# Expert gates placed among the late blocks of the first table, and three regroupings in a second block

## The chip, the cores and the metric

One core of a Trainium2 chip. The metric is device time in microseconds (us) for one execution, the median of three. TensorE is PE in the profile (PEld its weight loads), VectorE is DVE, ScalarE is ACT, GpSimd is POOL, SyncE is SP.

## What is computed

Two transformer-like blocks over 256 tokens of width 1024, all in float32. The first ends in a feed-forward part with 16,384 experts: each token takes 8 x 16 of them, and an expert is a pair of keys (i1, i2), each of 0 to 127.

```python
expert = i1 * N_KEYS + i2
gate = jax.nn.softmax(best_s, axis=-1)
act = jax.nn.gelu(jnp.einsum('nd,ned->ne', hx, u[expert]))
return jnp.einsum('ne,ned->nd', gate * act, v[expert])
```

The second begins with one projection `h @ w_in` that is cut into a recurrent branch (`rx`, `rgate`, 2 x 1344 columns), sparse attention's q, k and v, its 48 gate columns `nsa_g` (3 for each of 16 heads, through a sigmoid), and two mixing gates. Sparse attention also compresses windows of 32 positions: `gelu((windows + pe) @ w1) @ w2`, for k and for v.

## The kernel before, in words

**Weights** come as one stream of 512 KB quarters through a ring of four (`ring`). SP loads a quarter when its slot is free. For most of them ACT rounds it to float32r (`round_quarter`, L824, its instruction L829), POOL takes the rest (`lower_quarter`, L1687), and PE multiplies three products: high by high, high by low, low by high (`product`, L318, instructions L323 to L325). SPLIT names the quarters treated so; others are multiplied as float32 (L321).

**The expert part** computes all experts for all tokens. The first table (u) is 128 quarters, called blocks: block m holds the experts with i2 = m, i1 on partitions, and `peer_u` (L613) multiplies it with all 256 tokens, 24 matmuls of 256 columns. Two blocks fill one PSUM bank, four banks (0 to 3) go round, and ACT's `gelu_u` (L962, L968) takes a bank to `region`, which holds activations [i1, block, token]. Beside the first U_EARLY = 80 blocks DVE finds each token's 128 slots (top keys, top pairs; L1390 to L1427); ACT's exponential for the softmax (L980) stands behind those 80 blocks on ACT's queue. Then PE turns the slots (L632), so that i1, i2 and the gate lie [slot, token] in banks 6 and 7, DVE copies them to `slotT` (L1432), and the other 48 blocks follow.

Only then come the **gates**, in 64 groups of 4 tokens. For a token a 128 x 128 matrix of gates is a matmul (float32, L646) of a one-hot matrix of i1 (ACT: four squares L991 and a relu L995) with one of i2 times the gate (DVE, L1444). DVE multiplies the result into `region` (`weigh`, L1453). X serves as buffer for the one-hot matrices; it is written out to HBM before and read back after.

Then the second table (v), 128 blocks: ACT rounds the activations (L1010), DVE takes the rest (L1476), PE multiplies (`peer_v`, L656).

**The second block.** 32 recurrent blocks of 84 columns (`feature_major`, L462, 24 matmuls of 256 columns each); the last two carry 24 gate columns each, which PE multiplies token-major (L323 to L325 with 24 columns) into bank 7. Then nine blocks z0 to z8 of 512 columns (`z2`, L722; `token_major`, L443, 48 matmuls each), which ACT keeps (L1082). After z5, ACT takes the sigmoid of the gates (L1092) and squares q and k (L1096 to L1098), DVE sums them (L1535), ACT takes the root (L1100), DVE scales q into N2 (L1544), and PE turns it (`transposes`, L420, instruction L425). The same buffer is filled and turned for k during z6 (L1554) and for the compressed k and v during z7 (L1562). After z8 PE multiplies the compression weights with the windows (L747, 60 columns: 4 groups of 15 windows) and separately with the position vector (L751, 1 column).

Every engine works through its own queue in the order written; waits are on semaphores.

## Time and profile before

| | |
|---|---|
| median of three runs | 1992.43 us (1988.84 to 1996.98) |
| the profiled execution | 1988.24 us, span 1986.5 us |
| PE busy | 1684.7 us, 85% of the span |
| DVE busy | 1091.3 us, 55% |
| ACT busy | 889.9 us, 45% |
| POOL busy | 1143.9 us, 58% |
| weights streamed | 536 quarters of 512 KB |

The span is the time from the first to the last instruction; the execution's own time has 1.7 us more around it. Matmuls overlap, so PE's busy time tells when it has work, and the pace is read from counts over a stretch. The granted clock of TensorE is a share of 2.4 GHz: 1.00 or 0.50 at any moment, a mean over a stretch. A releaser (`<-`) is what ended the idle time in front of an instruction.

### The profile page before, as it was taken

The page shows a single profiled execution, that of the slowest core. Times are in us where ns is not written, and L with a number is a line of the kernel's source. Part 1 is how long each engine was busy: PE and PEld are TensorE (multiplying, and loading weights), DVE is VectorE, ACT ScalarE, POOL GpSimd, SP SyncE. Part 2 cuts the span into 40 slices and gives each one's busy share as a digit, 9 for nine tenths or more (in the row PEclk, how much of TensorE's full clock was granted, in tenths as well). Part 3 has the DMA queues.
Part 4 walks back from the last instruction along what each step waited for, and adds up shares of the span by engine and source line. Part 5 has one row for each costly group of instructions (what it writes and reads, how often), then busy time and mean ns, then how long its engine had stood idle before and what let it go on. Part 6 is the DMA issues. An engine that isn't in the chain of part 4 may idle for free.

```text
span 1986.5 us, 28971 instructions
## 1 busy us (share of the span) xinstructions
PE 1684.7 (85%) x10051; PEld 1443.1 (73%) x10051; DVE 1091.3 (55%) x1650; ACT 889.9 (45%) x1456; POOL 1143.9 (58%) x482
## 2 busy tenths in 40 slices
PE   2775786999999996579999997799979888687878
PEld 2553444999999995568888886799859754487867
DVE  6677323599700008878888886735161571345453
ACT  1333202555555559975455543375553350233232
POOL 0658102789986880028888885756943400275676
PEclk9898767999999999999999998898987999788989
DMA  7674213455455550015555554444533203243443
GB/s 260 218 248 165 75 50 117 152 182 179 168 190 174 186 184 27 0 43 190 193 195 194 190 192 153 147 163 138 189 117 119 104 1 116 96 156 119 151 144 131
DMA packets 79490, 288.75 MB, mean 145 GB/s; under 512 B 8769, under 2 KB 9281, under 8 KB 79298
## 3 DMA queue, kind: packets, MB, share of 16 engines
q1 hardware_dynamic: 78160, 283.51, 41.3%
q10 hardware_dynamic: 1266, 4.36, 0.7%
q8 instruction: 43, 0.70, 0.1%
q14 instruction: 21, 0.17, 0.0%
HBM read 285.75 MB, written 2.10 MB: 145 GB/s over the span
## 4 chain that ended last, share of the span: by engine, by line
PE 71%; DVE 9%; ACT 7%; POOL 5%; issue 3%; DMA 3%; ACTq 1%; SPq 0%; DVEq 0%; POOLq 0%
PE PS L323 20%; PE PS L325 19%; PE PS L324 19%; PE PS L321 6%; POOL low L1687 5%; ACT X L991 4%; DMA ring<-in_stream 3%; PE PS L425 1%; ACT high L829 1%; DVE hTl L1172 1%; DVE hTh L1171 1%; PE PS L694 1%; DVE region L1265 1%; ACT region L877 1%; PE PS L523 1%
## 5 line engine op out<-in xcount | busy, mean ns | idle before, releaser
L1687 POOL TENSOR_TENSOR low<-ring,high 128x1024 fp32r<-128x1024 f32 x448 | 1102.0, 2476 | 825.5 <-ACT high L829 824.8
L829 ACT ACTIVATE high<-ring 128x1024 fp32r<-128x1024 f32 x448 | 471.3, 1058 | 504.8 <-PE PS L325 405.6
L323 PE MATMUL PS<-hTh,high 128*128 128x256 f32 (+1 forms) x1728 | 500.1, 289 | 66.1 <-POOL low L1687 36.7
L324 PE MATMUL PS<-hTl,high 128*128 128x256 f32 (+1 forms) x1728 | 497.6, 288 | 0.0
L325 PE MATMUL PS<-hTh,low 128*128 128x256 f32 (+1 forms) x1728 | 496.8, 288 | 0.0
L323 PE MATMUL PS<-high,hTh 128*128 128x512 f32 (+1 forms) x960 | 378.9, 395 | 39.7 <-POOL low L1687 20.1
L323 PEld LDWEIGHTS PS<-hTh,high 128*128 128x128 f32 (+1 forms) x1728 | 331.4, 192 | 69.5 <-DVE hTl L1172 29.0
L324 PE MATMUL PS<-low,hTh 128*128 128x512 f32 (+1 forms) x960 | 374.7, 390 | 0.0
L325 PE MATMUL PS<-high,hTl 128*128 128x512 f32 (+1 forms) x960 | 374.4, 390 | 0.0
L324 PEld LDWEIGHTS PS<-hTl,high 128*128 128x128 f32 (+1 forms) x1728 | 331.5, 192 | 0.1
L325 PEld LDWEIGHTS PS<-hTh,low 128*128 128x128 f32 (+1 forms) x1728 | 331.0, 192 | 0.0
L1476 DVE TENSOR_TENSOR hTl<-region,hTh 128x256 fp32r<-128x256 f32 x128 | 289.1, 2260 | 57.2 <-ACT hTh L1010 57.2
L323 PEld LDWEIGHTS PS<-high,hTh 128*128 128x128 f32 x960 | 184.4, 192 | 86.2 <-POOL low L1687 25.7
L325 PEld LDWEIGHTS PS<-high,hTl 128*128 128x128 f32 x960 | 184.1, 192 | 37.7
L324 PEld LDWEIGHTS PS<-low,hTh 128*128 128x128 f32 x960 | 184.5, 192 | 36.4
L1444 DVE TENSOR_SCALAR X<-iota,slotT 128x128 f32<-128x128 f32 x256 | 71.1, 341 | 139.6 <-ACT region L968 139.6
L646 PE MATMUL PS<-X 128*128 128x128 f32 x512 | 76.6, 295 | 49.3 <-ACT X L995 49.3
L321 PE MATMUL PS<-ring,region 128*128 128x512 f32 x256 | 113.0, 603 | 3.2 <-DVE region L1194 1.7
L646 PEld LDWEIGHTS PS<-X 128*128 128x128 f32 x512 | 64.4, 197 | 61.5 <-ACT X L995 61.2
L1265 DVE SCALAR_TENSOR_TENSOR region<-ring,cols,region 128x512 f32<-128x512 f32 x70 | 85.8, 1225 | 27.0 <-DMA ring<-in_stream 24.3
L321 PEld LDWEIGHTS PS<-ring,region 128*128 128x128 f32 x256 | 49.1, 193 | 65.1 <-issue 60.6
L991 ACT ACTIVATE X<-iota,slotT 128x128 f32<-128x128 f32 x256 | 80.8, 386 | 0.6 <-PE PS L646 0.6
(256 smaller groups left out, 1443.0 us busy)
## 6 DMA issues: line engine op xcount, KB each, us to landing
ring<-in_stream SPq DMA_DIRECT2D x536, 512.0 KB, 3.2
X<-in_x SPq DMA_DIRECT2D x1, 1024.0 KB, 5.0
region<-in_band ACTq DMA_DIRECT2D x1, 1024.0 KB
result<-X ACTq DMA_DIRECT2D x1, 1024.0 KB, 5.8
X<-result ACTq DMA_DIRECT2D x1, 1024.0 KB, 4.9
result<-X SPq DMA_DIRECT2D x1, 1024.0 KB, 4.0
region<-in_skeys ACTq DMA_DIRECT2D x1, 512.0 KB
region<-in_consts ACTq DMA_DIRECT2D x1, 352.0 KB, 2.8
```

Of the source, the lines that this page charges most:

```text
L321: return pe.matmul(out_, stat, mov, start=start, stop=stop, **kw)
L323: pe.matmul(out_, sh, mh, start=start, stop=False, **kw)
L324: pe.matmul(out_, sh, ml, start=False, stop=False, **kw)
L325: return pe.matmul(out_, sl, mh, start=False, stop=stop, **kw)
L425: last = pe.transpose(PS[:, c // 2, (c % 2) * S + t * P:(c % 2) * S + (t + 1) * P], src[:, t, c * P:(c + 1) * P], ident[:, :])
L646: last = pe.matmul(PS[:, g % 2, j * P:(j + 1) * P], onehot[:, 0, g % 2, j, :], onehot[:, 1, g % 2, j, :], start=True, stop=True)
L829: act.activation(high[:, b % RING, :], ring[:, b % RING, :], ACT.Copy).then_inc(rounded[b % RING], 1)
L991: act.activation(onehot[:, 0, g % 2, j, :], iota[:, :], ACT.Square, bias=slotT[:, 0, bass.ds(4 * g + j + 8 * r, 1)]).then_inc(sem("rows_sq ...
L1265: ins = dve.scalar_tensor_tensor(ada_acc(j), w[:, c, :], col("cT", 2 * q + c), ada_acc(j), ALU.mult, ALU.add)
L1444: last = dve.tensor_scalar(onehot[:, 1, g % 2, j, :], iota[:, :], slotT[:, 1, n], slotT[:, 2, n], ALU.is_equal, ALU.mult)
L1476: dve.tensor_tensor(lo, src, hi.bitcast(F32), ALU.subtract).then_inc(sem("weights_split"), 1)
L1687: pool.tensor_tensor(low[:, b % RING, :], ring[:, b % RING, :], high[:, b % RING, :].bitcast(F32), ALU.subtract).then_inc(left[b % RING], 1)
```

## The change

**Gates among late blocks.** U_EARLY becomes 64, and ACT's exponential moves in front of the last 16 of these. The other 64 blocks are written out one by one, and behind each PE places the gates of one group of 4 tokens, in banks 4 and 5. One-hot matrices are float32r in buffers of their own (`onehot`, and `gate2` as `second`); the gate is split in two parts, so a token takes two float32r matmuls. The slots stay in PSUM, and DVE compares from there, 4 tokens in one instruction. ACT scales one matrix by the rest of the gate (`second_rest`). DVE's `weigh` multiplies the blocks that are done, and copies the gates to the place of those that are not; for a late pair of blocks ACT applies gelu inside PSUM for tokens whose gates have been placed and DVE multiplies (`weigh_late`), and for the other tokens it writes `region`, to be multiplied later. X is no longer moved out and back.

**Sparse attention's gates.** The 48 columns become rows 96 to 119 of the last two recurrent blocks' products. ACT copies them, PE turns them with four transposes behind z1, and ACT copies them to NSG; the sigmoid moves behind z8.

**Squares beside projections.** ACT squares q behind z2 and k behind z4, and takes the root in front of z5's copies.

**Positions as a column group.** The position vector becomes a fifth group of columns beside the four of windows (75 columns in one matmul), filled by DVE with a memset and two copies of 16 elements.

```diff
-slotT = sb("slotT", [P, 3, S])
+onehot = sb("onehot", [P, 3, 2, NB], F32R)
+gate_rest = sb("gate_rest", [P, S])
...
-U_EARLY = 80
-take = carve(U_EARLY * S)
+U_EARLY = 64
+GROUPS = S // 4
+take = carve(80 * S)
...
-onehot = X[:, :, :].rearrange("p t d -> p (t d)").rearrange("p (w g j k) -> p w g j k", w=2, g=2, j=4)
+second = gate2.rearrange("p (b n) -> p b n", b=2)
+act_v = region[:, :].rearrange("p (i n) -> p i n", n=S)
+def fours(buf):
+    return buf.rearrange("p (j k) -> p j k", j=4)
+def blocks_done(g):
+    return U_EARLY + 2 * (g // 2)
...
+GATE_ROWS = slice(96, 96 + GATES // 2)
+GATE_IN = XN2.rearrange("p t d -> p (t d)")[:, 0:2 * S].rearrange("p (k s) -> p k s", k=2)
...
-    with pe.Fori(U_EARLY // 8, NK // 8) as r:
-        for k in range(8):
-            peer_u(k, r)
-    def gates(g, r=0):
-        pe.wait_ge(sem("first_rows_ready"), g + 1 + 2 * r)
-        pe.wait_ge(sem("second_rows_ready"), g + 1 + 2 * r)
-        pe.wait_ge(sem("gate_banks_free"), g + 1 + 2 * r)
+    def gates(g):
+        pe.wait_ge(sem("rows_ready"), g + 1)
+        pe.wait_ge(sem("rest_ready"), g + 1)
+        if g >= 2:
+            pe.wait_ge(sem("gates_used"), g - 1)
+        rows, high_, rest = (fours(onehot[:, w, g % 2, :]) for w in range(3))
         for j in range(4):
-            last = pe.matmul(PS[:, g % 2, j * P:(j + 1) * P], onehot[:, 0, g % 2, j, :],
-                             onehot[:, 1, g % 2, j, :], start=True, stop=True)
+            dst = PS[:, 4 + g % 2, j * P:(j + 1) * P]
+            pe.matmul(dst, rows[:, j, :], high_[:, j, :], start=True, stop=False)
+            last = pe.matmul(dst, rows[:, j, :], rest[:, j, :], start=False, stop=True)
         last.then_inc(sem("gates_placed"), 1)
-    pe.sem_inc(sem("gates_placed"), 1)
-    with pe.Fori(0, S // 8) as r:
-        for g in range(2):
-            gates(g, r)
+    for g in range(GROUPS):
+        peer_u(U_EARLY + g)
+        gates(g)
+    pe.wait_ge(sem("u_banks_free"), 4 + NK // 2)
...
-        ins = feature_major(name, q, RW, PS[0:RW, i % 4, 0:S])
-        k = i - (2 * RB - 2)
-        if k == 0:
+        width = RW if i < 2 * RB - 2 else GATE_ROWS.stop
+        free_slot(name, q, feature_major(name, q, width, PS[0:width, i % 4, 0:S]))
+    def z2(i):
+        if i == 0:
             pe.wait_ge(sem("rgate_kept"), 2 * RB)
-        if k >= 0:
-            w = slot(name, q, P)
-            for t in range(T):
-                for c in range(KC):
-                    ins = product(pe, PS[:, 7, t * HD + k * GATES // 2:t * HD + (k + 1) * GATES // 2],
-                                  hT[:, c, t * P:(t + 1) * P], w[:, c, RW:RW + GATES // 2],
-                                  start=(c == 0), stop=(c == KC - 1))
-        free_slot(name, q, ins)
-    def z2(i):
-        if i == 1:
-            pe.wait_ge(sem("r_kept"), RB + T)
         elif i >= 2:
             pe.wait_ge(sem("z2_kept"), 2 * (i - 1))
         token_major(f"z{i}", hT, lambda t, o: 4 + (2 * i + t) % 4)
     for i in range(6):
         z2(i)
+        if i == 1:
+            pe.wait_ge(sem("gates_kept"), 2)
+            pe.wait_ge(sem("r_kept"), RB)
+            for t in range(T):
+                for k in range(2):
+                    last = pe.transpose(PS[:, 2, (2 * t + k) * 32:(2 * t + k) * 32 + GATES // 2],
+                                        GATE_IN[GATE_ROWS, k, t * P:(t + 1) * P],
+                                        ident[GATE_ROWS, GATE_ROWS])
+            last.then_inc(sem("gates_turned"), 1)
+    pe.wait_ge(sem("gates_kept"), 3)
...
-            pe.matmul(PS[:, kv, 0:KV * NCMP], w[:, l % (CLEN // 4), :],
-                      CT2[:, KV * kv:KV * (kv + 1), 2 * l:2 * l + CSTEP * (NCMP - 1) + 1:CSTEP],
-                      start=(l == 0), stop=(l == CLEN // 2 - 1))
-        for l in ls:
-            last = pe.matmul(PS[:, 2 + kv, 0:1], w[:, l % (CLEN // 4), :],
-                             col("pek" if kv == 0 else "pev", l), start=(l == 0), stop=(l == CLEN // 2 - 1))
+            last = pe.matmul(PS[:, kv, 0:(KV + 1) * NCMP], w[:, l % (CLEN // 4), :],
+                             CT2[:, kv, :, 2 * l:2 * l + CSTEP * (NCMP - 1) + 1:CSTEP],
+                             start=(l == 0), stop=(l == CLEN // 2 - 1))
...
-    with act.Fori(0, U_EARLY // 8) as r:
+    with act.Fori(0, U_EARLY // 8 - 2) as r:
         for k in range(0, 8, 2):
             gelu_u(k, r)
-    act.dma_start(out.rearrange("(t p) d -> p t d", p=P), X[:, :, :]).then_inc(sem("x_moved"), 16)
     act.wait_ge(sem("best_less_max"), 1)
     act.activation(BE.rearrange("p t h k -> p (t h k)"), BE.rearrange("p t h k -> p (t h k)"),
                    ACT.Exp).then_inc(sem("best_exp"), 1)
-    act.wait_ge(sem("slots_saved"), 3)
-    with act.Fori(U_EARLY // 8, NK // 8) as r:
+    with act.Fori(U_EARLY // 8 - 2, U_EARLY // 8) as r:
         for k in range(0, 8, 2):
             gelu_u(k, r)
-    def first_rows(g, r=0):
-        if not (isinstance(r, int) and g < 2):
-            act.wait_ge(sem("gates_placed"), g + 2 * r)
+    def second_rest(g):
+        act.wait_ge(sem("second_ready"), g + 1)
         for j in range(4):
-            act.activation(onehot[:, 0, g % 2, j, :], iota[:, :], ACT.Square,
-                           bias=slotT[:, 0, bass.ds(4 * g + j + 8 * r, 1)]).then_inc(sem("rows_squared"), 1)
-        act.wait_ge(sem("rows_squared"), 4 * (g + 1) + 8 * r)
-        rows = onehot[:, 0, g % 2, :, :].rearrange("p j k -> p (j k)")
-        act.activation(rows, rows, ACT.Relu, scale=-1.0,
-                       bias=ones[:, 0:1]).then_inc(sem("first_rows_ready"), 1)
-    act.wait_ge(sem("x_moved"), 16)
-    first_rows(0)
-    with act.Fori(0, S // 8 - 1) as r:
-        first_rows(1, r)
-        first_rows(2, r)
-    first_rows(S // 4 - 1)
+            ins = act.activation(fours(onehot[:, 2, g % 2, :])[:, j, :], fours(second[:, g % 2, :])[:, j, :],
+                                 ACT.Copy, scale=gate_rest[:, 4 * g + j:4 * g + j + 1])
+        ins.then_inc(sem("rest_ready"), 1)
+    def gelu_late(p):
+        m = U_EARLY + 2 * p
+        b = QUARTERS * AT["u0"] + m + 1
+        act.wait_ge(multiplied[b % RING], nth_split(b))
+        n = 8 * (p + 1)
+        src = PS[:, m % 8 // 2, :].rearrange("p (w s) -> p w s", w=2)
+        if n < S:
+            act.activation(act_v[:, m:m + 2, n:S], src[:, :, n:S], ACT.Gelu)
+        act.activation(src[:, :, 0:n], src[:, :, 0:n], ACT.Gelu).then_inc(sem("late_gelu"), 1)
+    second_rest(0)
+    for g in range(GROUPS):
+        round_quarter(QUARTERS * AT["u0"] + U_EARLY + g + 3)
+        if g + 1 < GROUPS:
+            second_rest(g + 1)
+        if g % 2:
+            gelu_late(g // 2)
...
+        if i >= 2 * RB - 2:
+            act.activation(GATE_IN[GATE_ROWS, i - 2 * RB + 2, :], PS[GATE_ROWS, i % 4, 0:S],
+                           ACT.Copy).then_inc(sem("gates_kept"), 1)
...
-    for t in range(T):
-        act.activation(NSG[:, t, :], PS[:, 7, t * HD:t * HD + GATES], ACT.Copy).then_inc(sem("r_kept"), 1)
     def z2(i):
         wait_product(f"z{i}")
         for t in range(T):
     for i in range(2):
         z2(i)
         for j in (2 * i, 2 * i + 1):
-            act.wait_ge(sem("r_kept"), RB + T)
+            act.wait_ge(sem("r_kept"), RB)
             act.activation(four(RGT, j), four(RGT, j), ACT.Gelu_apprx_tanh).then_inc(sem("rec_gelu"), 1)
-    for i in range(2, 6):
-        z2(i)
-    act.activation(NSG[:, :, :], NSG[:, :, :], ACT.Sigmoid)
-    act.wait_ge(sem("z2_kept"), 10)
-    act.wait_ge(sem("rec_out"), 1)
-    for t in range(T):
-        act.activation(SQ2[:, t, 0:1024], Z2[:, t, 0:1024], ACT.Square).then_inc(sem("sq2"), 1)
-        act.activation(SQ2[:, t, 1024:1280], Z2[:, t, KS2:KS2 + 256], ACT.Square).then_inc(sem("sq2"), 1)
-        act.activation(SQ2[:, t, 1280:1536], Z2[:, t, KW2:KW2 + 256], ACT.Square).then_inc(sem("sq2"), 1)
+    act.wait_ge(sem("root_tanh"), 4)
+    def squares(o, src, n, blocks):
+        act.wait_ge(sem("z2_kept"), 2 * blocks)
+        for t in range(T):
+            act.activation(SQ2[:, t, o:o + n], Z2[:, t, src:src + n], ACT.Square).then_inc(sem("sq2"), 1)
+    z2(2)
+    act.wait_ge(sem("gates_turned"), 1)
+    act.activation(NSG.rearrange("p t (k n) -> p (t k) n", k=2),
+                   PS[:, 2, 0:128].rearrange("p (u n) -> p u n", u=4)[:, :, 0:GATES // 2],
+                   ACT.Copy).then_inc(sem("gates_kept"), 1)
+    squares(0, 0, 1024, 2)
+    z2(3)
+    z2(4)
+    squares(1024, KS2, 256, 4)
+    squares(1280, KW2, 256, 5)
+    ahead("z5", 1)
     act.wait_ge(sem("qk2_meansq"), 2)
     act.activation(st2[:, 1, :], st2[:, 0, :], ACT.Sqrt).then_inc(sem("qk2_root"), 1)
+    z2(5)
...
+    act.wait_ge(sem("gates_kept"), 3)
+    act.activation(NSG[:, :, :], NSG[:, :, :], ACT.Sigmoid).then_inc(sem("gates_kept"), 1)
...
-    for w in range(3):
-        dve.tensor_scalar(slotT[:, w, :], PS[:, 6 + w // 2, (w % 2) * S:(w % 2 + 1) * S],
-                          -1.0 if w == 0 else 1.0, None, ALU.mult).then_inc(sem("slots_saved"), 1)
-    dve.wait_ge(sem("slots_saved"), 3)
-    dve.sem_inc(sem("gate_banks_free"), 2)
-    def rows(g, r=0):
-        if not (isinstance(r, int) and g < 2):
-            dve.wait_ge(sem("gates_placed"), g + 2 * r)
-        for j in range(4):
-            n = bass.ds(4 * g + j + 8 * r, 1)
-            last = dve.tensor_scalar(onehot[:, 1, g % 2, j, :], iota[:, :], slotT[:, 1, n], slotT[:, 2, n],
-                                     ALU.is_equal, ALU.mult)
-        last.then_inc(sem("second_rows_ready"), 1)
-    act_v = region[:, :].rearrange("p (i n) -> p i n", n=S)
-    def weigh(g, r=0):
-        dve.wait_ge(sem("gates_placed"), g + 2 + 2 * r)
-        v = act_v[:, :, bass.ds(4 * g + 8 * r, 4)]
-        dve.tensor_tensor(v, v, PS[:, g % 2, :].rearrange("p (n i) -> p i n", n=4),
-                          ALU.mult).then_inc(sem("gate_banks_free"), 1)
+    gate_high = onehot[:, 2, 0, 0:S]
+    link(dve.tensor_copy(gate_high, PS[:, 7, 0:S]))
+    link(dve.tensor_tensor(gate_rest[:, :], PS[:, 7, 0:S], gate_high.bitcast(F32), ALU.subtract))
+    link(dve.tensor_copy(PS[:, 7, S:2 * S], gate_high.bitcast(F32)))
+    def rows(g):
+        i1, i2, gate = PS[:, 6, 0:S], PS[:, 6, S:2 * S], PS[:, 7, S:2 * S]
+        tok = slice(4 * g, 4 * g + 4)
+        keys = bc(iota[:, :], 1, 4)
+        if g >= 2:
+            dve.wait_ge(sem("gates_placed"), g - 1)
+        dve.tensor_tensor(fours(second[:, g % 2, :]), keys, bc(i2[:, tok], 2, P),
+                          ALU.is_equal).then_inc(sem("second_ready"), 1)
+        dve.tensor_tensor(fours(onehot[:, 0, g % 2, :]), keys, bc(i1[:, tok], 2, P), ALU.is_equal)
+        dve.wait_ge(sem("second_ready"), g + 1)
+        dve.tensor_tensor(fours(onehot[:, 1, g % 2, :]), fours(second[:, g % 2, :]), bc(gate[:, tok], 2, P),
+                          ALU.mult).then_inc(sem("rows_ready"), 1)
+    def weigh(g):
+        dve.wait_ge(sem("gates_placed"), g + 1)
+        n = blocks_done(g)
+        v, placed = act_v[:, :, 4 * g:4 * g + 4], PS[:, 4 + g % 2, :].rearrange("p (n i) -> p i n", n=4)
+        dve.tensor_tensor(v[:, 0:n, :], v[:, 0:n, :], placed[:, 0:n, :], ALU.mult)
+        dve.tensor_copy(v[:, n:NK, :], placed[:, n:NK, :]).then_inc(sem("gates_used"), 1)
+    def weigh_late(p):
+        m, n = U_EARLY + 2 * p, 8 * (p + 1)
+        dve.wait_ge(sem("late_gelu"), p + 1)
+        dve.wait_ge(sem("gates_used"), 2 * p + 2)
+        v = act_v[:, m:m + 2, 0:n]
+        dve.tensor_tensor(v, v, PS[:, m % 8 // 2, :].rearrange("p (w s) -> p w s", w=2)[:, :, 0:n],
+                          ALU.mult).then_inc(sem("u_banks_free"), 1)
+    rows(0)
+    rows(1)
+    dve.wait_ge(sem("u_banks_free"), 4 + U_EARLY // 2)
+    for g in range(GROUPS):
+        weigh(g)
+        if g % 2:
+            weigh_late(g // 2)
+        if g + 2 < GROUPS:
+            rows(g + 2)
     dve.wait_ge(sem("u_banks_free"), 4 + NK // 2)
-    dve.wait_ge(sem("x_moved"), 16)
-    rows(0)
-    with dve.Fori(0, S // 8 - 1) as r:
-        rows(1, r)
-        weigh(0, r)
-        rows(2, r)
-        weigh(1, r)
-    rows(S // 4 - 1)
-    weigh(S // 4 - 2)
-    weigh(S // 4 - 1)
-    dve.wait_ge(sem("gate_banks_free"), 2 + S // 4)
...
+    link(dve.memset(CT2[:, :, KV, :], 0.0))
+    for kv, name in enumerate(("pek", "pev")):
+        o, n = COL[name]
+        link(dve.tensor_copy(CT2[:, kv, KV, 0:2 * n:2], cols[:, o:o + n]))
```

The layout of the weights on the host and the indices of CT2 follow from this.

## Rows read from the trace of the kernel before

**Rows 1.** The page: busy time of each engine, share of span, instructions.
```profile
PE 1684.7 (85%) x10051; PEld 1443.1 (73%) x10051; DVE 1091.3 (55%) x1650; ACT 889.9 (45%) x1456; POOL 1143.9 (58%) x482
```

**Rows 2.** Stretches: length, busy PE, PEld, DVE, ACT, POOL; clock, DMA share, GB/s.
```profile
556.20:602.30 46.10, 46.10 (x386) 46.00 (x384) 0.00 (x0) 25.99 (x28) 38.13 (x17) 1.00 0.53 183
...
607.90:748.10 140.20, 139.80 (x1152) 139.60 (x1150) 0.95 (x3) 77.75 (x84) 113.83 (x48) 0.99 0.52 176
748.10:877.40 129.30, 78.36 (x528) 66.16 (x529) 110.84 (x322) 123.58 (x327) 0.35 (x1) 0.97 0.02 6
...
1355.00:1375.30 20.30, 20.30 (x143) 20.20 (x142) 20.13 (x18) 5.40 (x9) 8.07 (x3) 0.77 0.30 102
1375.30:1388.00 12.70, 12.70 (x49) 10.28 (x48) 8.14 (x6) 5.26 (x7) 8.73 (x4) 0.83 0.27 92
...
1432.40:1443.10 10.70, 10.70 (x48) 8.63 (x46) 0.00 (x0) 5.20 (x6) 9.81 (x5) 1.00 0.62 206
1443.10:1456.30 13.20, 0.16 (x2) 0.04 (x1) 6.58 (x7) 7.29 (x12) 1.01 (x1) 0.68 0.19 72
...
1498.70:1522.40 23.70, 23.70 (x129) 23.70 (x128) 3.73 (x4) 9.25 (x8) 6.70 (x3) 0.58 0.19 67
```

**Rows 3.** Groups by line, 740 to 900 us: busy, mean ns, idle before, releaser.
```profile
L991 ACT ACTIVATE X<-iota,slotT 128x128 f32<-128x128 f32 x256 | 80.8, 386 | 0.6 <-PE PS L646 0.6
L646 PE MATMUL PS<-X 128*128 128x128 f32 x512 | 76.6, 295 | 49.3 <-ACT X L995 49.3
...
L1453 DVE TENSOR_TENSOR region<-region,PS 128x512 f32 x62 | 42.6, 687 | 14.2 <-PE PS L646 14.1
L1687 POOL TENSOR_TENSOR low<-ring,high 128x1024 fp32r<-128x1024 f32 x12 | 28.7, 2396 | 135.1 <-ACT high L829 135.1
```

**Rows 4.** Timeline of PE at the end of the gates: start, duration.
```profile
872.38 1.16 PE L646 MATMUL PS<-X 128*128 128x128 f32 x8 [0.77 <-ACT X L995]
...
877.43 0.47 PE L323 MATMUL PS<-high,hTh 128*128 128x512 f32 x1 [2.10 <-DVE hTl L1476]
```

**Rows 5.** Groups by line, 330 to 740 us (the blocks of the first table).
```profile
L829 ACT ACTIVATE high<-ring 128x1024 fp32r<-128x1024 f32 x133 | 139.0, 1055 | 59.2 <-PE PS L325 55.6 <-DMA ring<-in_stream 3.0
L968 ACT ACTIVATE region<-PS 128x512 f32 x62 | 37.1, 599 | 86.8 <-PE PS L325 86.6
...
L968 ACT ACT_TABLE_LOAD x16 | 20.5, 1283 | 30.7 <-PE PS L325 30.7
```

**Rows 6.** Timeline of PE at 207.7 us, granted clock 0.5: start, duration.
```profile
207.72 0.69 PE L496 MATMUL PS<-hTl,identr 128*128 128x128 f32 x2
208.21 0.65 PE L507 MATMUL PS<-ident,region 128*128 128x128 f32 x2
```

**Rows 7.** Single lines of DVE: count, ns min/median/max, first and last start.
```profile
L1661 DVE SCALAR_TENSOR_TENSOR region<-PS,cols,region x48: 482/482/484, 1734.8 to 1921.3; 128x255 f32<-128x255 f32 x48
...
L1670 DVE TENSOR_TENSOR region<-region x24: 424/426/2266, 1755.4 to 1922.4; 128x256 f32<-128x256 f32 x24
...
L1172 DVE TENSOR_TENSOR hTl<-region,hTh x8: 1225/2234/3245, 51.3 to 1719.6; 128x1024 fp32r<-128x1024 f32 x8
...
L1562 DVE COPY region<-region x8: 280/1321/2380, 1474.6 to 1483.1; 128x256 f32<-128x256 f32 x8
```

**Rows 8.** Timeline of DVE around the routing of experts.
```profile
470.80 1.07 DVE L1405 TENSOR_TENSOR region<-region 128x256 f32<-128x256 f32 x1
...
533.65 2.29 DVE L1422 TENSOR_REDUCE region<-region 128x128 f32<-128x2048 f32 x1
...
604.96 0.42 DVE L1425 TENSOR_REDUCE region<-region 128x16 f32<-128x256 f32 x1 [69.03 <-ACT region L980]
```

**Rows 9.** Groups by line, 1230 to 1560 us (second block).
```profile
L747 PE MATMUL PS<-region,ring 128*128 128x60 f32 x64 | 12.6, 373 | 0.0
...
L751 PE MATMUL PS<-cols,ring 128*128 128x1 f32 x64 | 12.4, 324 | 0.0
...
L1535 DVE TENSOR_REDUCE region<-region 128x48 f32<-128x3072 f32 x1 | 3.4, 3352 | 41.3 <-ACT region L1098 41.3
```

26 lines of the change are left out of this document (13 added, 13 removed).

## The prediction

> **What bounds the kernel now.** I read the page first: PE is busy for 85% of the span, POOL 58%, DVE 55%, ACT 45% [rows 1]. A gain must come from stretches where PE is idle or multiplies little. Stretches show where these are. In the first table PE runs at full clock with a matmul every 0.12 us: 386 in 46.10 us, so a block of 24 costs 2.88 us, and the 48 blocks behind the routing take 140.20 us [rows 2]. From 748.1 to 877.4 us PE is busy for 78 of 129 us, POOL and DMA stand still, and ACT (123.6 us) sets the pace [rows 2]; the groups say the same: PE waited 49.3 us for ACT's one-hot rows [rows 3]. In the second block three stretches stand out: 20.30 us around the last two recurrent blocks, 13.20 us with PE empty while ACT and DVE normalise q, and 23.70 us of small matmuls at a mean clock of 0.58 [rows 2].
>
> **The first table and the gates.** From the start of block 64 (556.2 us) to v's first matmul (877.4 us) the kernel takes 321.2 us: 16 blocks, the routing's stall, 48 blocks, the gates. Afterwards it holds 64 blocks and 64 groups, and the slowest engine per pair of groups sets the pace.
>
> PE: two blocks, 5.76 us, and 16 float32r matmuls of 128 columns. None of that shape runs at full clock before. The nearest row is two of them at clock 0.5, where the next instruction starts 0.49 us after the first [rows 6]: 0.245 us each, 0.12 at full clock. Upwards the bound is the float32 one: a group's four matmuls appear as 8 records in 1.16 us [rows 4], 0.29 us each; downwards 0.10 us, a little under the 0.12 of the blocks' matmuls, which load as many weights [rows 2]. I take 0.12, the same type and shape: 0.96 us a group, 3.84 with its block, 7.7 us a pair.
>
> DVE, a pair: six comparisons and products of 512 elements, two `weigh` in two pieces, one `weigh_late` (264 elements on average). The nearest is the old `weigh`, 0.687 us for 512 from region and PSUM [rows 3]: 6 x 0.687 + 2 x 0.84 + 0.4 = 6.2 us. ACT, a pair: two roundings of 1.055 [rows 5], eight scaled copies of 128 elements at 0.386 [rows 3], a gelu of 0.599 in two pieces, about 0.8 [rows 5]: 6.0 us. POOL: 2 x 2.40 [rows 3] = 4.8 us. All below 7.7, so PE sets the pace and these cost nothing, as long as they run at these durations; if DVE or ACT grows by more than 1.5 us a pair, the excess is paid 32 times. The waits have room too: from a placed group through `weigh`, the comparison, ACT's scaling to the group two later is about 0.7 + 0.7 + 1.5 us, and PE takes over 6 us to come there.
>
> What DVE's durations are beside POOL decides. With one operand in PSUM, 48 instructions of the last stage took 482 to 484 ns [rows 7]; with both inputs in SBUF, 24 of the same stage took 424 to 2266 ns [rows 7], and the subtraction of 1024 elements 1225 to 3245 [rows 7]. Every comparison, product and copy per group has its slots, gates or products in PSUM, so I take the undisturbed durations. The Trainium skill (GPSIMD Engine Reference, Key points) states that GpSimd's SBUF interfaces are contended by DVE instructions with two SBUF inputs or in a 2-port mode; by that rule the loop is free of it, but not the q normalisation and the small copies below.
>
> Around the loop: turning the slots and the first comparisons, some 1.6 us. ACT's exponential is no longer late: DVE is through with its first part at 471.9 us and the routing at 536 [rows 8], the exponential comes near 510 and block 64 at 556, so the 69 us that DVE waited [rows 8] and PE's stall go. At the end, 5.1 us lie between the start of the last gates and v's first product [rows 4]; the last two weighings now come before the gate's spreading, so 6 us from the last gates' end. X's transfers ran beside other work: nothing. Sum: 64 x 3.84 + 1.6 + 6 = 253.4 against 321.2: **-67.8 us**. Bounds: 0.10 gives -78, 0.29 gives +19.
>
> **Gates as rows.** 20.30 us become 48 matmuls of 0.12, 5.8 us: -14.5. z0 behind it took 12.70 us at mean clock 0.83, z5 10.70 at full clock [rows 2]; the clock fell during the 24-column matmuls, so I expect -2.0 more. Four transposes, +0.5. ACT's copies have slack (5.40 us busy of 20.30 [rows 2]). **-16.0**, between -13 and -17.
>
> **Squares beside projections.** Behind z5 PE is empty for 13.20 us [rows 2]. Now DVE's sum of 3.35 us [rows 9] starts about 2.8 us behind z4's end (two copies like L968's 0.6 [rows 5], four short squares like L991's 0.39 [rows 3]); with the means, the root and the reciprocal, some 0.3 each, it is at 7.3, and two scalings of 1.225 to 3.245 each [rows 7] end at 9.8 to 13.8; z5 ends at 10.7. Both inputs in SBUF, and POOL is at work now: I take 2 us left. **-11.2**, between -10 and -13. Late next is this scaling.
>
> **Positions as columns.** The 64 one-column matmuls are half the matmuls of 23.70 us and half their time (12.4 of 25.0 [rows 9]): -11.8. Wider columns beside them cost nothing: 60 columns and one take the same time. Behind, the next quarters must be loaded, rounded (1.055 [rows 5]) and lowered (2.40 [rows 3]) sooner; a quarter or so may be late and keep up to 4 us. In front, DVE has a memset and two copies more before PE may turn the windows. DVE is late there already; eight copies took 280 to 2380 ns each, median 1.32 [rows 7]: 2 x 1.3 + 0.3 = +3, between +0.7 and +5. Together **-8.8**, between -3 and -12.
>
> **Sum:** -67.8 - 16.0 - 11.2 - 8.8 = -103.8. The profiled execution took 1988.24 us (span 1986.5); it becomes 1884.4. The median shown is 4.2 us above it: 1888 us.
>
> **Rivals.** (a) The float32r gate matmuls cost what float32 ones do, 0.29: 64 x 8 x 0.17 = +87, 1975 us. For it: the shape was never seen at full clock. Against: 0.245 at half clock, and the same at 0.29 would need 0.58. (b) One wait turns it slower: DVE waits for POOL in each of its 11 instructions a pair, as the two-input ones do. DVE stands in front of `gates_used` and `rows_ready`, and everything behind. The old stretch gives (321.2 - 7.6)/32 = 9.8 us a pair, 10.9 with the second block's 36 us; DVE reaches it when each waits 0.43 us. At the full 2266 - 424 = 1.84 us a pair takes 26.4 us: 32 x 26.4 = 846 against 321, 2477 us. Against: 48 rows without any such wait. (c) The second block's 36 us come only by half, because the ring, POOL or the scalings are next: 1906 us. (d) ACT reloads its tables in the loop: the old loop had 16 loads in each direction for 62 gelus, 1.283 us each [rows 5]. If each pair had both, ACT would need 6.0 + 2.6 = 8.6 us a pair, 0.9 over PE: +29, 1917 us. Against: loads came once per turn of a loop, and this one is written out. (e) The matmul is cheaper: 0.06 us for 128 columns, 64 x 8 x 0.06 = -31, 1857 us. Against: one-column matmuls with fresh weights were no faster than 60-column ones [rows 9]. The Trainium skill (VectorE: DVE Perf Modes, the section on the TRN2 errata) gives a matmul max(60, 6 + columns) cycles, 134 for 128 columns, 0.056 us; by the trace weights of 128 columns bound it before.
>
> **Chances.** Forecast 0.70 (1872 to 1905), (a) 0.06, (b) 0.04, (c) 0.10, (d) 0.06, (e) 0.04. A difference of 0.5%, 10 us, is about what can be told from none. Faster: all but (b), and a little for mixtures: 0.95; same 0.01; slower 0.04. The range takes the forecast, (c) and (d), and stops short of (e), (a), (b): 1862 to 1920.
>
> **What would show it.** A stretch of 64 equal pieces of about 3.84 us with clock 1.00, PE without idle, POOL at 2.4 of 3.84 us, DVE busy about 80%; DVE's `rows` at 0.69 us, not 2; gate matmuls 0.12 us apart; no table load inside. No 24-column matmuls; PE idle behind z5 for 0 to 3 us; the turn of the windows later by about 3; 64 compression matmuls instead of 128. Wrong if the pieces are over 4.9 us, or if DVE's comparisons stretch while POOL works.

## The result and the profile after

The changed kernel takes **1886.84 us** (median of 3 runs, 1885.93 to 1889.74) against 1992.43: a ratio of 0.947, 95% interval 0.944 to 0.951. The profiled execution took 1885.93 us. The forecast was 1888 us, but one of its four terms, the squares, came out at a fifth of its size or less; two others and a stretch that varies from run to run covered for it.

The page of the kernel after, span and busy time of each engine (beside [rows 1]):

```profile
span 1884.1 us, 27492 instructions
PE 1632.5 (87%) x9895; PEld 1402.6 (74%) x9895; DVE 1201.7 (64%) x1685; ACT 827.9 (44%) x1407; POOL 1158.9 (62%) x482
```

Stretches of the kernel after (length, busy PE, PEld, DVE, ACT, POOL, then clock, DMA share, GB/s): inside the late blocks, DVE's recurrent chain, the hole behind z5, the compression:

```profile
565.00:785.00 220.00, 220.00 (x1877) 220.00 (x1877) 161.45 (x323) 150.67 (x350) 140.91 (x60) 1.00 0.41 142
...
1276.30:1339.40 63.10, 62.13 (x293) 50.10 (x292) 62.86 (x23) 39.34 (x48) 61.51 (x22) 1.00 0.50 175
...
1351.60:1362.50 10.90, 0.53 (x3) 0.56 (x4) 9.72 (x8) 3.10 (x5) 4.83 (x3) 0.69 0.20 63
...
1408.50:1417.90 9.40, 7.98 (x61) 7.75 (x60) 3.54 (x5) 8.02 (x9) 2.45 (x2) 0.96 0.51 174
```

The late blocks are as dense as the blocks were before [rows 2]. PE's timeline there (start, duration, idle before) shows the matmul on which the forecast hung: a gate matmul every 0.11 us at clock 1.00.

```profile
552.78 0.82 PE L645 MATMUL PS<-ident,region 128*128 128x128 f32 x6
...
700.17 0.28 PE L658 MATMUL PS<-onehot 128*128 128x128 f32 x1
700.28 0.27 PE L657 MATMUL PS<-onehot 128*128 128x128 f32 x1
700.39 0.27 PE L658 MATMUL PS<-onehot 128*128 128x128 f32 x1
...
796.36 2.05 PE L681 MATMUL PS<-ident,adaT 128*128 128x128 f32 x16 [1.64 <-DVE region L1483]
800.51 0.47 PE L336 MATMUL PS<-high,hTh 128*128 128x512 f32 x1 [2.10 <-DVE hTl L1502]
```

From the slots' transposes to v's first matmul: 247.7 us, where the stretch of [rows 4] ended 321.2 us after block 64's start. Single lines of DVE and ACT in it (count, ns min/median/max):

```profile
L1464 DVE TENSOR_TENSOR gate<-iota,PS x64: 676/678/686, 555.0 to 788.7; 128x512 f32<-128x512 f32 x64
L1466 DVE TENSOR_TENSOR onehot<-iota,PS x64: 678/680/682, 555.6 to 789.3; 128x512 fp32r<-128x512 f32 x64
L1468 DVE TENSOR_TENSOR onehot<-gate,PS x64: 677/679/681, 556.2 to 789.9; 128x512 fp32r<-128x512 f32 x64
L993 ACT ACTIVATE onehot<-gate,gate_rest x256: 384/388/406, 555.7 to 790.3; 128x128 fp32r<-128x128 f32 x128
```

Two slots of every comparison in PSUM, 64 times and never a wait for POOL. In the second block it is otherwise. The 16 scans of the recurrence and the eight copies that fill c2's input, whose inputs all lie in SBUF:

```profile
L1551 DVE TENSOR_TENSOR_SCAN region<-region x16: 657/2818/2835, 1277.5 to 1336.6; 84x256 f32<-84x256 f32 x16
...
L1587 DVE COPY region<-region x8: 280/1318/2376, 1381.4 to 1390.0; 128x256 f32<-128x256 f32 x8
```

The same scans had a median of 663 ns before. From the kernel before:

```profile
L1526 DVE TENSOR_TENSOR_SCAN region<-region x16: 656/663/2818, 1356.0 to 1381.5; 84x256 f32<-84x256 f32 x16
```

And the timeline of the kernel after around the hole behind z5, ACT first, then DVE, then PE:

```profile
1340.24 1.34 ACT L1105 ACTIVATE region<-region 128x256 f32<-128x256 f32 x4
...
1356.43 0.24 ACT L1119 ACTIVATE region<-region 128x48 f32<-128x48 f32 x1 [11.66 <-DVE region L1564]
```
```profile
1336.61 2.81 DVE L1551 TENSOR_TENSOR_SCAN region<-region 84x256 f32<-84x256 f32 x1
1339.46 13.26 DVE L1555 TENSOR_TENSOR region<-region 84x1024 f32<-84x1024 f32 x4
1352.75 3.35 DVE L1560 TENSOR_REDUCE region<-region 128x48 f32<-128x3072 f32 x1
...
1357.19 4.51 DVE L1569 TENSOR_TENSOR region<-region 128x1024 f32<-128x1024 f32 x2
```
```profile
1159.83 3.68 PE L438 MATMUL PS<-ident,region 128*128 128x128 f32 x16 [10.88 <-DVE region L1186]
...
1361.97 3.65 PE L438 MATMUL PS<-ident,region 128*128 128x128 f32 x16 [10.61 <-DVE region L1572]
```

The squares are done at 1341.6, ten microseconds before z5 is. DVE does not take them: it is in its chain, from 1276 on without a pause, until 1352.75. PE's hole behind z5 is 10.6 us; it was 13.0 us in the kernel before.

Where the 102.4 us of span went, each by the starts of the same instructions in both traces: up to the slots' transposes -3.4; first table from block 64 to v -73.5; v's stage -1.6; from the transposes with which the second block begins (n3's, at 1159.83 above) to q's (projections, recurrence, hole) 217.96 to 202.14, -15.8, of which the hole is 2.4; q's transposes to the first matmul of the output, ro0, 66.1 to 56.0, -10.2; the rest +2.1. The first of these varies from run to run: in a second profile of the changed kernel that instant came 4 us earlier still (548.8), with the stretches behind it alike to 0.1 us.

### The profile page after: what moved, and what is told of

Read it like the earlier page. It is cut to its first block, busy times and chain, and to the rows that moved or that the text cites. A ratio compares the mean times of both kernels' runs of the same rounds, so it can differ in the third digit from the quotient of the medians.

```text
span 1884.1 us, 27492 instructions
## 1 busy us (share of the span) xinstructions
PE 1632.5 (87%) x9895; PEld 1402.6 (74%) x9895; DVE 1201.7 (64%) x1685; ACT 827.9 (44%) x1407; POOL 1158.9 (62%) x482
## 4 chain that ended last, share of the span: by engine, by line
PE 73%; DVE 14%; POOL 5%; ACT 4%; issue 2%; DMA 2%; ACTq 0%; SPq 0%; DVEq 0%; POOLq 0%
PE PS L336 20%; PE PS L337 19%; PE PS L338 19%; PE PS L334 6%; POOL low L1717 5%; DMA ring<-in_stream 2%; DVE region L1551 2%; PE PS L658 2%; PE PS L657 1%; PE PS L438 1%; ACT high L837 1%; DVE hTl L1194 1%; DVE region L1287 1%; DVE hTh L1193 1%; PE PS L705 1%
## 5 line engine op out<-in xcount | busy, mean ns | idle before, releaser
L1717 POOL TENSOR_TENSOR low<-ring,high 128x1024 fp32r<-128x1024 f32 x448 | 1116.4, 2505 | 707.4 <-ACT high L837 707.0
L336 PE MATMUL PS<-hTh,high 128*128 128x256 f32 (+1 forms) x1728 | 500.3, 290 | 66.1 <-POOL low L1717 36.7
L336 PE MATMUL PS<-high,hTh 128*128 128x512 f32 x928 | 370.2, 399 | 40.4 <-POOL low L1717 20.3
L337 PE MATMUL PS<-low,hTh 128*128 128x512 f32 x928 | 365.6, 394 | 0.0
L338 PE MATMUL PS<-high,hTl 128*128 128x512 f32 x928 | 365.1, 393 | 0.0
L336 PEld LDWEIGHTS PS<-high,hTh 128*128 128x128 f32 x928 | 176.9, 191 | 89.8 <-POOL low L1717 27.0
L337 PEld LDWEIGHTS PS<-low,hTh 128*128 128x128 f32 x928 | 177.0, 191 | 35.3
L993 ACT ACTIVATE onehot<-gate,gate_rest 128x128 fp32r<-128x128 f32 x256 | 82.0, 391 | 66.6 <-DVE gate L1464 66.6
L1689 DVE TENSOR_SCALAR region<-PS,cols 128x256 f32<-128x256 f32 x48 | 26.0, 541 | 87.4 <-PE PS L338 84.7
L438 PE MATMUL PS<-ident,region 128*128 128x128 f32 x176 | 35.0, 382 | 49.6 <-DVE region L1186 27.3
L1475 DVE TENSOR_TENSOR region<-region,PS 128x256 f32<-128x256 f32 (+31 forms) x64 | 35.2, 551 | 61.1 <-PE PS L658 61.1
```

Of the source, the lines that this page charges most:

```text
L336: pe.matmul(out_, sh, mh, start=start, stop=False, **kw)
L337: pe.matmul(out_, sh, ml, start=False, stop=False, **kw)
L338: return pe.matmul(out_, sl, mh, start=False, stop=stop, **kw)
L438: last = pe.transpose(PS[:, c // 2, (c % 2) * S + t * P:(c % 2) * S + (t + 1) * P], src[:, t, c * P:(c + 1) * P], ident[:, :])
L993: ins = act.activation(fours(onehot[:, 2, g % 2, :])[:, j, :], fours(second[:, g % 2, :])[:, j, :], ACT.Copy, scale=gate_rest[:, 4 * g + j ...
L1717: pool.tensor_tensor(low[:, b % RING, :], ring[:, b % RING, :], high[:, b % RING, :].bitcast(F32), ALU.subtract).then_inc(left[b % RING], 1)
```

## The experiments

**Theory 1**: the rows and the squares are not separate savings. The 24-column matmuls kept PE busy while POOL had little to split; DVE's chain of two-input instructions ran in that time. Without them it runs beside a busy POOL, takes almost twice as long, and is what PE waits for behind z5. **Theory 2**: the hole is the squares' own (their order on ACT, the scaling behind them, the clock), and terms add up. For the first table, that PE alone bounds it, against DVE being close, and that the operand's place decides DVE's durations.

All figures "n3 to q" are starts of PE's rows as quoted above, and "hole" is the idle time in brackets on q's row. The expectations count the hole from the start of the last product, 0.4 us more.

### Undoing the terms

**undo_rows.** The gates come back as 24-column products; squares and positions stay as changed.

```diff
-                width = RW if i < 2 * RB - 2 else GATE_ROWS.stop
-                free_slot(name, q, feature_major(name, q, width, PS[0:width, i % 4, 0:S]))
+                ins = feature_major(name, q, RW, PS[0:RW, i % 4, 0:S])
...
+                            ins = product(pe, PS[:, 7, t * HD + k * GATES // 2:t * HD + (k + 1) * GATES // 2],
+                                          hT[:, c, t * P:(t + 1) * P], w[:, c, RW:RW + GATES // 2],
+                                          start=(c == 0), stop=(c == KC - 1))
+                free_slot(name, q, ins)
```

> The changed kernel with sparse attention's gates again as 24-column products between the last recurrent blocks; the squares beside the projections and the position columns stay. Theory 1, rows and squares interact: the 24-column matmuls (some 16 us) come back, but GpSimd idles under them, VectorE's scans run uncontended (1.3 us each instead of 2.7), the recurrent chain is over long before the last projection and TensorE's gap before q's transposes shrinks from 11.0 us to 0 to 3: 1886.8 + 16 - 9 = about 1893 (1891 to 1896). Theory 2, the gap is the squares' own (their waits and the scaling behind them): it stays at 10 to 12 us, and the kernel takes 1901 to 1904.

**undo_squares.** The squares go behind z5's copy and the recurrent output.

```diff
-            squares(0, 0, 1024, 2)
-            z2(3)
-            z2(4)
-            squares(1024, KS2, 256, 4)
-            squares(1280, KW2, 256, 5)
-            ahead("z5", 1)
+            for i in range(3, 6):
+                z2(i)
+            act.wait_ge(sem("rec_out"), 1)
+            squares(0, 0, 1024, 5)
+            squares(1024, KS2, 256, 5)
+            squares(1280, KW2, 256, 5)
```

> The changed kernel with the squares again behind the last projection and the recurrent output; rows and position columns stay. Theory 1: VectorE's chain ends at the same time as in the changed kernel and only the squares and their reduction come behind it: the gap before q's transposes grows from 11.0 to 14 to 16 us, 1890 to 1892. Theory 2, terms that add up as forecast (squares worth 11 us): 1897 to 1899.

**undo_both.** Both edits together.

> Both undone; the first table and the position columns stay as changed. Both theories: the gap before q's transposes is 13.4 us as in the kernel before and the 24-column matmuls are back: 1886.8 + 15.8 + 2.4 = 1905 (1903 to 1907). Under theory 1 the squares are then worth 11 to 13 us with the 24-column matmuls there (this kernel less undo_rows) and 3 to 5 us without them (undo_squares less the changed kernel); under theory 2 the two differences are alike.

Measured (q's row of PE in each trace, in the order undo_rows, undo_squares, undo_both; n3's transposes started at 1160.69, 1156.59, 1164.25):

```profile
1369.70 3.11 PE L438 MATMUL PS<-ident,region 128*128 128x128 f32 x16 [2.88 <-DVE region L1567]
```
```profile
1360.15 3.24 PE L438 MATMUL PS<-ident,region 128*128 128x128 f32 x16 [11.91 <-DVE region L1571]
```
```profile
1380.70 3.67 PE L438 MATMUL PS<-ident,region 128*128 128x128 f32 x16 [11.44 <-DVE region L1566]
```

| n3 to q, us (hole) | 24-column products | gates as rows | rows are worth |
|---|---|---|---|
| squares behind | 216.45 (11.4) | 203.56 (11.9) | 12.9 |
| squares beside | 209.01 (2.9) | 202.14 (10.6) | 6.9 |
| squares are worth | 7.4 | 1.4 | |

The medians are 1893.1, 1883.1 and 1899.7 us on a chip where the kernel before took 1985.7: ratios of 0.952 (0.950 to 0.955), 0.947 (0.945 to 0.950) and 0.955 (0.953 to 0.958). Their intervals are some 5 us wide each way. They tell undo_both from the changed kernel (0.944 to 0.951), while undo_rows's touches it and undo_squares's lies on it. So the comparison rests on the stretch inside the traces, one profile of each kernel; between two profiles of the changed kernel it repeats to 0.03 us (202.14, 202.17). By the expectations' count the holes are 3.3, 12.3 and 11.8 us, where theory 1 had 0 to 3, 14 to 16 and 13.4: right in kind, 0.3 to 1.7 us off. Theory 2's 10 to 12 for undo_rows is excluded. The squares' worth was expected at 11 to 13 us with the 24-column products and at 3 to 5 without them; it is 7.4 and 1.4, so theory 1 had the order right and both sizes too high. The two savings overlap by 6.0 us. The scans of undo_rows, with POOL idle for half the time (21.3 us busy of 44.0), against the 2818 above:

```profile
L1546 DVE TENSOR_TENSOR_SCAN region<-region x16: 656/688/2893, 1279.6 to 1310.4; 84x256 f32<-84x256 f32 x16
```
```profile
1276.80:1320.80 44.00, 43.88 (x243) 39.77 (x242) 35.32 (x25) 20.43 (x26) 21.32 (x10) 0.84 0.31 105
```

The same chain's end in undo_rows, and the sum that waits for z4's squares instead of for the chain:

```profile
1325.18 6.31 DVE L1550 TENSOR_TENSOR region<-region 84x1024 f32<-84x1024 f32 x2 [7.47 <-ACT region L1098]
1358.39 3.35 DVE L1555 TENSOR_REDUCE region<-region 128x48 f32<-128x3072 f32 x1 [26.90 <-ACT region L1105]
```

undo_rows brings two things back at once, and does not separate them: POOL's pause, and some 15 us of PE's time before z5's end. From its first product behind a root the chain takes 76.4 us in the changed kernel and 53.2 us in undo_rows, waits included. Two estimates from these rows: the slow chain of 76.4 us, started at 1278.3, would have been over at 1354.7 in undo_rows, still before the sum's start, so PE's time alone would have closed the hole as far; and a chain of 53.2 us would have been over by 1329.5 in the changed kernel, before z4's squares (1341.6), so there would have been no hole either. It takes both, a slow chain and projections that end sooner.

**undo_positions.** Separate one-column matmuls again, no position columns in CT2.

```diff
-                    last = pe.matmul(PS[:, kv, 0:(KV + 1) * NCMP], w[:, l % (CLEN // 4), :],
-                                     CT2[:, kv, :, 2 * l:2 * l + CSTEP * (NCMP - 1) + 1:CSTEP],
+                    pe.matmul(PS[:, kv, 0:KV * NCMP], w[:, l % (CLEN // 4), :],
+                              CT2[:, kv, 0:KV, 2 * l:2 * l + CSTEP * (NCMP - 1) + 1:CSTEP],
...
+                for l in ls:
+                    last = pe.matmul(PS[:, 2 + kv, 0:1], w[:, l % (CLEN // 4), :],
+                                     col("pek" if kv == 0 else "pev", l), start=(l == 0), stop=(l == CLEN // 2 - 1))
```

> The changed kernel with the positions again as one-column matmuls into a bank of their own. If the terms are what the two traces give: 64 matmuls back behind the compression's products, the compression takes 23 to 24 us instead of 8 to 9 and some 4 us at its end are given back, since the wait before ro0 (1.8 us) and the fill of CT2 (1.1 us) go: 1886.8 + 10 = 1897 (1894 to 1900). A rival, that the transfers or splits for ro0 set its start anyway: under 1890.

1897.8 us, ratio 0.954 (0.951 to 0.957). From q's transposes to ro0: 66.3 us instead of 56.0, so the term is worth 10.4 us; n3 to q is 202.2 as in the changed kernel. With the one-column matmuls there ro0 waits for nothing:

```profile
1429.96 3.51 PE L762 MATMUL PS<-cols,ring 128*128 128x1 f32 x16
1433.33 0.77 PE L336 MATMUL PS<-high,hTh 128*128 128x512 f32 x1
```

Without them, in the changed kernel, it waits 1.5 us for POOL's split:

```profile
1413.82 2.67 PE L758 MATMUL PS<-region,ring 128*128 128x75 f32 x19
1417.95 0.76 PE L336 MATMUL PS<-high,hTh 128*128 128x512 f32 x1 [1.47 <-POOL low L1717]
```

### Shortening what theory 1 names

**products_later.** Two of the four gating products move behind c2's kept halves.

```diff
-            for j in range(4):
-                dve.wait_ge(sem("rec_gelu"), j + 1)
-                ins = dve.tensor_tensor(four(XC, j), four(XC, j), four(RGT, j), ALU.mult)
-            ins.then_inc(sem("rec_out"), 1)
+            def gated(js):
+                for j in js:
+                    dve.wait_ge(sem("rec_gelu"), j + 1)
+                    ins = dve.tensor_tensor(four(XC, j), four(XC, j), four(RGT, j), ALU.mult)
+                ins.then_inc(sem("rec_out"), 1)
+
+            gated((0, 1))
...
+            gated((2, 3))
+            dve.wait_ge(sem("rec_out"), 2)
             for i in range(2):
                 split_fours("ro", XC, i, f"z{Z2B - 1}", RW)
```

> The changed kernel with two of the four gating products of the recurrent output (84x1024, 3.4 us each beside GpSimd) moved behind the kept halves of c2, where VectorE has 7.8 us idle. Theory 1, VectorE's chain alone holds the scaling back: the chain ends 6.7 us sooner, TensorE's gap before q's transposes goes from 11.0 to 4 to 5 us, the products disappear in the idle time, and the kernel is 6 us faster than the changed one: a ratio of 0.944 to the kernel before, against 0.947. Theory 2, ScalarE (z5's copy, the squares) or the clock holds it back: the gap stays at 10 us or more.

The hole falls from 10.6 to 5.0 us, n3 to ro0 from 258.1 to 251.0. By the expectations' count the hole is 5.4 us, against 4 to 5; 1879.7 us, ratio 0.946 (0.942 to 0.949), an interval that overlaps the changed kernel's. Theory 2 had 10 or more. Counted from n3's transposes the reduction starts 5.5 us sooner and q's transposes 4.5; z5 ends 1.1 us later.

**roots_sooner.** Four decays, tanhs and roots to a block on ACT.

```diff
-                if k < 6:
-                    for n in range(3 * k, min(3 * k + 3, RB)):
+                if k < 4:
+                    for n in range(4 * k, 4 * k + 4):
                         decay(n)
...
-                    j = k - 12
+                    j = k - 8
```

> The changed kernel with the decays, tanhs and square roots packed four to a recurrent block instead of three, so that the roots for which VectorE's chain waits 17.8 us come four blocks (some 12 us) sooner. Theory 1: the chain ends some 12 us sooner, the gap before q's transposes falls from 11.0 to 0 to 2 us, and n3's transposes to q's take 191 to 194 us instead of 202.2; ratio 0.941 to 0.943. Theory 2 as in products_later: the gap stays. A miss of another kind: ScalarE, at 3.4 us a block against TensorE's 3.3, delays the recurrent blocks by what the chain gains.

The hole falls to 4.5 us, not to 0 to 2, and n3 to q to 199.7, not 191 to 194. Three things took the difference. The chain's first product behind a root started 7.9 us sooner, not 12, and from there the chain took 65.3 us instead of 63.2, so the reduction came 5.8 us sooner. From the reduction's start to the transposes it was 12.6 us instead of 9.2, with 2.42 us for a 128x16 operation and 1.24 for a 128x32 one that take 0.17 and 0.18 in the changed kernel. And up to z5's end PE took 3.6 us more: it waits for POOL in the projections, and POOL has DVE in its way for longer. n3 to ro0 takes 253.1 us, 5 less, which the whole run is too coarse to show (1882.9 us, 0.948, 0.945 to 0.951). A miss in size, and the first sign that a stall moved on DVE comes back in part beside POOL.

### What bounds the late blocks

**one_product.** The gates' lower part is left out of the product; everything that prepares it stays.

```diff
-                    pe.matmul(dst, rows[:, j, :], high_[:, j, :], start=True, stop=False)
-                    last = pe.matmul(dst, rows[:, j, :], rest[:, j, :], start=False, stop=True)
+                    last = pe.matmul(dst, rows[:, j, :], high_[:, j, :], start=True, stop=True)
```

> The changed kernel without the second of the two gate products of each token (the gates' lower part is left out; its copies on ScalarE are still made). If TensorE bounds the late blocks, a group falls from 3.75 us to 3.75 - 4 x 0.11 = 3.31 and the first table from block 64 from 247.7 to about 220 us. If VectorE or ScalarE (5.5 and 5.1 us busy a pair of groups in the trace) is nearly a bound too, less than half of that comes. The rival with 0.056 us a gate matmul (from the width of the operand alone) would give half: 234 us.

One execution took 1861.1 us. Slots' transposes to v's first matmul, 220.7 us:

```profile
558.54 0.82 PE L645 MATMUL PS<-ident,region 128*128 128x128 f32 x6
...
779.27 0.77 PE L336 MATMUL PS<-high,hTh 128*128 128x512 f32 x1 [2.10 <-DVE hTl L1501]
```

256 matmuls fewer take 27.0 us off, 0.105 each where 0.11 was expected: nearly all of it shows, so PE sets the pace. At 0.056 us each it would have been 14 us, which is excluded.

**second_in_sbuf.** The row that the second comparison reads is copied to SBUF once.

```diff
+            link(dve.tensor_copy(slot_in[:, :], PS[:, 6, S:2 * S]))
...
-                i1, i2, gate = PS[:, 6, 0:S], PS[:, 6, S:2 * S], PS[:, 7, S:2 * S]
+                i1, i2, gate = PS[:, 6, 0:S], slot_in, PS[:, 7, S:2 * S]
```

> The changed kernel with the second slot's row, which one of the three comparisons of a group reads, in SBUF instead of PSUM, so that this 128x512 instruction has both operands in SBUF while GpSimd splits weights. If an operand in PSUM is what kept VectorE free of GpSimd, this one alone goes from 680 ns to 1.2 to 2.4 us and the other two stay at 680; VectorE then needs 6.5 to 9 us for a pair of groups against TensorE's 7.5: up to 7.5 nothing is lost, at 9 the stretch grows by some 45 us. If the place of the operand doesn't matter, it stays at 680 ns.

Groups of 600 to 760 us (busy, mean ns); the comparison is L1466, its neighbours L1468 and L1470:

```profile
L1719 POOL TENSOR_TENSOR low<-ring,high 128x1024 fp32r<-128x1024 f32 x43 | 107.2, 2495 | 55.6 <-ACT high L838 54.9
...
L1466 DVE TENSOR_TENSOR gate<-iota,slot_in 128x512 f32<-128x512 f32 x43 | 59.4, 1382 | 0.0
...
L1468 DVE TENSOR_TENSOR onehot<-iota,PS 128x512 fp32r<-128x512 f32 x43 | 29.1, 676 | 0.0
L1470 DVE TENSOR_TENSOR onehot<-gate,PS 128x512 fp32r<-128x512 f32 x43 | 29.0, 675 | 0.0
```

In the mean the one instruction doubles, and the others keep their time. It is not slowed every time: of its 64 executions the median is 688 ns and the longest 2916, so about half met no split. DVE is then busy 200 of 220 us, still under PE, and the stretch takes 248.2 us against 247.7 (one execution: 1884.3 us). So the operand's place decides whether an instruction can be held up, and the loop had room for one such instruction a group. All three in SBUF were not tried.

### Towards a faster version

**changed_again**: the changed kernel, unedited, beside the two that follow.

> The changed kernel itself, as the yardstick on the same chip: ratio 0.947 to the kernel before, TensorE's gap before q's transposes 11.0 us, n3's transposes to q's 202 us.

1884.7 us, ratio 0.950 (0.948 to 0.951), hole 10.6, n3 to q 202.17.

**both_sooner**: the edits of products_later and roots_sooner together.

> The changed kernel with the roots four blocks sooner and two of the gating products behind c2's kept halves. By themselves the one took the start of the reduction 5.8 us earlier and the other 6.7 us (gaps of 4.9 and 5.4 us instead of 11.0). If VectorE's chain is the only thing before the scaling, both together end it 12.5 us sooner: the gap falls to 0 to 1.5 us, limited now by z4's squares and the 9 us of the scaling. What TensorE waits in the projections for GpSimd's splits (3.6 us more with the roots sooner) comes again. Net 7 to 8 us faster than the changed kernel. If the moved stall is all that a moved chain gives (GpSimd is the resource that both need), less than 4 us.

1879.1 us, ratio 0.947 (0.946 to 0.948), 5.5 us faster than the changed kernel where 7 to 8 were expected. The hole stays at 3.7 us where 0 to 1.5 were expected, n3 to ro0 takes 251.2 (258.2 in changed_again). The timeline of DVE shows what is next:

```profile
1334.54 6.59 DVE L1556 TENSOR_TENSOR region<-region 84x1024 f32<-84x1024 f32 x2
1345.57 3.35 DVE L1563 TENSOR_REDUCE region<-region 128x48 f32<-128x3072 f32 x1 [4.43 <-ACT region L1105]
1348.96 1.56 DVE L1565 TENSOR_SCALAR region<-region 128x32 f32<-128x32 f32 x1
1350.43 2.42 DVE L1567 TENSOR_SCALAR region<-region 128x16 f32<-128x16 f32 x1
1353.17 0.45 DVE L1570 RECIPROCAL region<-region 128x48 f32<-128x48 f32 x1 [0.31 <-ACT region L1119]
1353.65 4.51 DVE L1572 TENSOR_TENSOR region<-region 128x1024 f32<-128x1024 f32 x2
```

DVE now waits 4.4 us for z4's squares, and from their end to the transposes lie 13 us, against z5's 11: the limit that the prediction had put at this place, met only once the chain is out of the way. Behind products_later, roots_sooner's edit gave n3 to ro0 nothing (251.0 with products_later alone).

**shared_fill**: as both_sooner; four of the eight copies of c2's fill on ACT, and the position columns' memset and copies behind the release of c2.

```diff
             keep_turned("k2", KT2, lambda c: col("gainks"))
+            act.wait_ge(sem("turned"), turned_by("k2", KC // 2))
+            for t in range(T):
+                for dup in range(2):
...
+                    act.activation(dst, Z2[:, t, VC2:VC2 + 256].rearrange("p (g d) -> p g d", g=KV),
+                                   ACT.Copy).then_inc(sem("c2_filled"), 1)
             z2(7)
...
+            pe.wait_ge(sem("c2_filled"), 2 * T)
             transposes("c2", N2, "n2_filled", 3)
```

> As both_sooner, and of the eight copies that fill c2's input (1.3 us each beside GpSimd on VectorE) four go to ScalarE behind k2's kept halves, and the position columns' memset and two copies come after c2 is released. TensorE waits 3.1 us before c2's transposes in the changed kernel: with VectorE's part 6.5 us shorter that wait goes to 0.3 us, unless ScalarE's copies (about 0.5 us each, 2 us) delay z7's copy. 2 to 3 us faster than both_sooner; if the clock or ScalarE bounds there, the same.

**1873.2 us** (1872.6 to 1878.0), ratio 0.945 (0.944 to 0.947): 11.5 us faster than the changed kernel by the medians of the same chip, and the intervals of the ratios don't meet. PE has no idle time before c2's transposes (2.8 us in the changed kernel), and n3 to ro0 takes 248.3 us:

```profile
1386.27 1.91 PE L438 MATMUL PS<-ident,region 128*128 128x128 f32 x16
```

Of the 11.5 us, 9.9 are in this stretch (248.3 against 258.2). Against both_sooner the stretch is 2.9 us shorter, where 2 to 3 were expected; the medians differ by 5.9 us, but their intervals overlap.

**queries_first**: as shared_fill; the queries' means, root and reciprocal by themselves, and the keys' behind q's input.

```diff
-            dve.wait_ge(sem("sq2"), 3 * T)
-            link(dve.tensor_reduce(st2[:, 2, :], SQ2.rearrange("p t (h d) -> p (t h) d", d=HD), AX_X, ALU.add))
+            dve.wait_ge(sem("sq2"), T)
+            mean_squares(slice(0, H2), 1.0, HD * EPS)
...
+            dve.wait_ge(sem("sq2"), 3 * T)
+            mean_squares(slice(H2, 24), 1.0 / HD, EPS)
             keep_turned("q2", QT2, lambda c: col("gainq"))
```

> As shared_fill, with the mean squares of the queries' heads (whose squares are done two projections before z5's end) reduced, rooted and scaled by themselves, and those of the keys' heads behind q's input. In both_sooner and shared_fill the gap before q's transposes is still 4.1 us: the reduction starts at z4's last squares, 1346.06 in both_sooner, where VectorE's chain was over at 1341.6, and 13 us lie from there to the transposes. If those squares and the 24-head reduction hold it now, the queries' path starts at the chain's end, needs some 10 us and is over before z5: the gap goes to 0.2 to 1 us, at most 2 us of it come back before k's transposes; 2 to 4 us faster than shared_fill, ratio 0.943 to 0.9445. If GpSimd's splits slow each of the small operations to their own length (2.4 us, as the 128x16 one), the gap stays at 3 us or more.

```profile
1354.75 1.94 PE L438 MATMUL PS<-ident,region 128*128 128x128 f32 x16 [0.47 <-DVE region L1593]
1371.12 2.79 PE L438 MATMUL PS<-ident,region 128*128 128x128 f32 x16 [3.52 <-DVE region L1606]
```
```profile
1358.49 12.36 DVE L1604 TENSOR_TENSOR region<-region 128x256 f32<-128x256 f32 x8
```

The hole is gone (0.5 us), and 3.5 us come back before k's transposes: k's fill starts later and takes 12.4 us beside POOL. n3 to ro0 is 249.2 us, 0.9 more than in shared_fill, where 2 to 4 us less were expected. The kernel takes 1879.1 us on another chip (0.946, 0.944 to 0.949), which is not to be told from shared_fill. The stall moved one step on: DVE is busy beside POOL on both sides of the hole, and what it was spared before q's transposes it needed before k's.

## Why the prediction was right, and where it was wrong

**First table, forecast -67.8, measured -73.5.** Mechanism and bound as stated: PE paces, POOL at 141 us of 220, DVE at 73%, no table loads inside. The difference is the gate matmul, 0.11 us instead of 0.12: a group took 3.755 us, and (3.84 - 3.755) x 64 = 5.4 us. Taking it from two instructions at half clock served well; 0.29 and 0.06 are both excluded, the second by one_product. The Trainium skill (VectorE: DVE Perf Modes, the section on the TRN2 errata) gives a formula from which 0.056 us for 128 columns is an estimate; the trace has 0.11, and the measurement decides.

**Rival (b), DVE held by POOL,** was set aside because of the operands in PSUM, and second_in_sbuf shows that reason: 0.68 us with one operand there, 1.38 in the mean with none. Its price of 26.4 us a pair was too high all the same: it lets each of 11 instructions wait for a split, and a pair has only two. Two waits of at most 2.4 us each make 6.2 + 4.8 = 11.0 us (an estimate), some 110 us over the 64 groups and not 600.

**Gates as rows, forecast -16.0.** Outside the hole 13.4 us went, at the low end of the range: z2 to z4 now take 11.6 to 11.7 us each instead of 10.9 to 11.0, with waits for POOL's splits in them. But of the whole only 6.9 us remain with the squares beside (undo_rows against the changed kernel), since the rest comes back in the hole.

**Squares, forecast -11.2, measured -1.4 with the rows in place, -7.4 without them.** The step that failed: "Now DVE's sum of 3.35 us starts about 2.8 us behind z4's end". z4's squares were over at 1341.6, but the sum stands behind the recurrent chain on DVE, and started at 1352.75. I counted ACT's path to the sum and not DVE's own queue. The rest of that step was right: the scalings took 4.5 us. The same rule was applied where it saved the forecast, in the first table, and to the scalings, but not to the 28 two-input instructions that stand before the sum, although the stretch of the 24-column matmuls showed POOL busy for only 8.07 of 20.30 us [rows 2]. What the removal of those matmuls took away was DVE's quiet time, and with it some 15 us behind which the chain had been hidden; the hole needed both.

**Positions, forecast -8.8, measured -10.2 and -10.4 by undoing.** The fill cost 1.1 us, not 3: memset 0.48 and two copies of 0.2 met no split. At the end 1.5 us are waited for POOL, as foreseen.

**Sum.** -103.8 forecast, -102.4 measured. The squares were 8.8 us short (2.4 of the hole went instead of 11.2) and the rows 2.6. That was made up by the first table (5.7 more), the positions (1.4 more), v's stage (1.6) and 3.4 us ahead of the slots that vary from run to run, less 2.1 elsewhere. That the total came out within 1.4 us is luck, and no proof of its terms.

## What to carry to other kernels

Before adding two savings up, ask what each leaves idle and who lives on it: here slow, nearly idle work on PE was POOL's pause, POOL's pause was DVE's quiet time, and all of it hid DVE's chain. When work is moved before an instruction, follow both its inputs and what is queued on its own engine. And when DVE and POOL both work from SBUF, count DVE's instructions, not its elements. One operand in PSUM (second_in_sbuf, the other way round) or copies on ACT (shared_fill) helped here; fewer and larger instructions should by the same durations, but were not tried.

## What the runs showed of the hardware

An instruction of DVE with all its inputs in SBUF (other than the reduction below) pays, when it meets one of POOL's splits, at most one wait of a split, whatever its size. Scans of 256 elements went from 0.66 to 2.83 us, products of 1024 from 1.22 to 3.4, copies of 256 from 0.28 to 2.38: +2.1 to +2.2 each, a little less than a split of 2.4 us. POOL pays too: its splits took 2414 ns on average while DVE rested and 2987 beside the chain (kernel after, groups of 1240 to 1256 and of 1277 to 1352 us):

```profile
L1717 POOL TENSOR_TENSOR low<-ring,high 128x1024 fp32r<-128x1024 f32 x7 | 16.9, 2414 | 1.9 <-ACT high L837 1.8
```
```profile
L1717 POOL TENSOR_TENSOR low<-ring,high 128x1024 fp32r<-128x1024 f32 x25 | 73.7, 2987 | 2.7 <-ACT high L837 2.7
```

The extra 0.6 us is about one scan of DVE (0.66), and beside the chain DVE finished 27 instructions while POOL finished 25: the two engines take turns. The Trainium skill (SBUF — State Buffer, Who interferes with whom) calls the shared port pair an exclusive lock, held for a whole instruction by whoever came first; the durations above agree. No run took POOL's splits away, so POOL as the cause rests on these durations, beside and without splits, and on second_in_sbuf. Even a 128x16 operation took 2.42 us in both_sooner, where it took 0.17 in the changed kernel's hole. The reduction of one input (128x3072) kept its 3.35 us in every trace that has it, beside POOL or not.

The 16 transposes of q took 3.65 us at a granted clock of 0.50 behind the hole of 10.6 us, the same behind one of 3.7 us (both_sooner), and 1.94 us at 1.00 behind one of 0.5 us (queries_first): a hole can cost 1.7 us more than its length, a short one too. It need not: k's 16 took 1.94 us behind a hole of 1.6 us in the changed kernel.
